# Opening of a two-layer hybrid trunk: order of the first loads, and where the split x tiles and h are made

## The reference

```python
h = concatenate([meta, x])                      # (272, 1024)
for l in range(2):
    f = (silu(a @ w_gate) * (a @ w_up)) @ w_down        # a = rms_norm(h, ffn1_pre[l]); 1024 -> 2816 -> 1024
    h = h + 0.5 * rms_norm(f, ffn1_post[l])
    proj = rms_norm(h, mix_pre[l]) @ w_in[l]
    mix = [pool | short convolution | gated linear attention](proj) @ w_out[l]
    h = h + rms_norm(mix, mix_post[l])
    h = h + 0.5 * rms_norm(swiglu(rms_norm(h, ffn2_pre[l])), ffn2_post[l])
return h[16:]
```

## Time and profile before

| | |
|---|---|
| median of the runs | 1014.23 us |
| the profiled execution, its own time | 1014.0 us |
| its span, first to last instruction | 1012.2 us |
| mean granted TensorE clock | 0.998 |
| TensorE busy | 1001.2 us (99%), 8904 matmuls |
| VectorE busy | 628.4 us (62%) |
| ScalarE busy | 499.5 us (49%) |
| GpSimd busy | 259.9 us (26%) |
| share of TensorE in the chain that ended last | 96% |
| SyncE's first issues | x0 0.76, meta 1.72, x1 2.11, weights from 2.57 us |
| landings | meta 5.42, x1 7.21, first weight piece 7.95, unit 1 13.57 us |

### The profile page before, as it was taken

How to read it: one execution, slowest core, us unless ns; L and a number is a source line. 1 busy time by engine, 2 the same in 40 slices (tenths; PEclk the granted TensorE clock), 3 DMA queues, 4 the chain that set the end, 5 groups by cost and what they waited for, 6 DMA issues and landing times.

```text
span 1012.2 us, 21339 instructions
## 1 busy us (share of the span) xinstructions
PE 1001.2 (99%) x8904; PEld 977.9 (97%) x8904; DVE 628.4 (62%) x643; ACT 499.5 (49%) x564; POOL 259.9 (26%) x180
## 2 busy tenths in 40 slices
PE   8999999999999999999999999999999999999997
PEld 7999999999999999999999999999999999999885
DVE  5765453588967745544477455444889787555485
ACT  6553443566566544343555443435675665434331
POOL 0343330113401333330103333301125014333200
PEclk9999999999999999999999999999999999999999
DMA  9775535645454755436747654357453547666521
GB/s 312 222 225 166 163 131 187 217 128 166 127 168 151 232 185 166 130 115 194 227 129 227 190 167 130 114 190 231 127 167 127 173 146 250 186 189 203 189 82 42
DMA packets 164019, 173.87 MB, mean 172 GB/s; under 512 B 9454, under 2 KB 151014, under 8 KB 163958
## 3 DMA queue, kind: packets, MB, share of 16 engines
q1 hardware_dynamic: 162044, 171.28, 53.4%
q10 hardware_dynamic: 1914, 1.72, 0.6%
HBM read 171.91 MB, written 1.06 MB: 171 GB/s over the span
## 4 chain that ended last, share of the span: by engine, by line
PE 96%; DMA 1%; DVE 1%; ACT 1%; SPq 0%; issue 0%; ACTq 0%; POOL 0%; DVEq 0%; POOLq 0%
PE ps L1477 25%; PE ps L1479 25%; PE ps L1478 25%; PE ps L1509 2%; PE ps L1494 2%; PE ps L1510 2%; PE ps L1685 2%; PE ps L1684 2%; PE ps L1686 2%; PE ps L1618 2%; PE ps L1656 2%; PE ps L1657 2%; PE ps L1811 1%; DMA raw<-in_ffn_wu 1%; PE ps L1536 1%; DVE w_lo L896 0%
## 5 line engine op out<-in xcount | busy, mean ns | idle before, releaser
L896 DVE TENSOR_TENSOR w_lo<-raw,w_hi 128x2048 fp32r<-128x2048 f32 (+2 forms) x174 | 383.8, 2210 | 269.1 <-ACT w_hi L578 268.5
L1477 PE MATMUL ps<-x_hi,w_hi 128*128 128x272 f32 (+2 forms) x1608 | 462.2, 287 | 0.7 <-DVE w_lo L896 0.7
L1479 PE MATMUL ps<-x_hi,w_lo 128*128 128x272 f32 (+2 forms) x1608 | 460.3, 286 | 0.0
L1478 PE MATMUL ps<-x_lo,w_hi 128*128 128x272 f32 (+2 forms) x1584 | 453.1, 286 | 0.0
L578 ACT ACTIVATE w_hi<-raw 128x2048 fp32r<-128x2048 f32 (+2 forms) x174 | 310.9, 1790 | 202.7 <-PE ps L1479 143.7
L1477 PEld LDWEIGHTS ps<-x_hi,w_hi 128*128 128x128 f32 x1608 | 302.8, 188 | 3.2 <-DVE w_lo L896 1.1
L1479 PEld LDWEIGHTS ps<-x_hi,w_lo 128*128 128x128 f32 x1608 | 302.3, 188 | 0.0
L1478 PEld LDWEIGHTS ps<-x_lo,w_hi 128*128 128x128 f32 x1584 | 298.3, 188 | 0.0
L1391 POOL TENSOR_TENSOR up<-gate,up 128x544 f32<-128x544 f32 (+1 forms) x44 | 59.4, 1350 | 311.8 <-ACT gate L713 311.8
L1394 POOL TENSOR_TENSOR hid_lo<-up,hid_hi 128x544 f32 (+3 forms) x44 | 122.4, 2782 | 45.5 <-ACT hid_hi L717 45.5
L713 ACT ACTIVATE gate<-gate 128x544 f32<-128x544 f32 (+1 forms) x44 | 28.7, 653 | 197.2 <-DVE gate L1112 197.2
(11 more groups left out here) (233 smaller groups left out, 1103.4 us busy)
## 6 DMA issues: line engine op xcount, KB each, us to landing
raw<-in_ffn_wg SPq DMA_DIRECT2D x87, 512.0 KB, 4.0
raw<-in_ffn_wu SPq DMA_DIRECT2D x87, 512.0 KB, 4.9
raw<-in_ffn_wd SPq DMA_DIRECT2D x72, 384.0 KB, 3.2
raw<-in_w_in SPq DMA_DIRECT2D x40, 512.0 KB, 4.6
raw<-in_ffn_wd SPq DMA_DIRECT2D x20, 512.0 KB, 4.7
raw<-in_ffn_wd SPq DMA_DIRECT2D x28, 256.0 KB, 3.3
raw<-in_w_out SPq DMA_DIRECT2D x12, 512.0 KB, 4.9
raw<-in_w_out SPq DMA_DIRECT2D x8, 256.0 KB, 3.9
```

The costliest lines, as they stand in the source:

```text
L896: v_.tensor_tensor(w_lo[:, slot, 0:n], raw[:, slot, 0:n], f32(w_hi[:, slot, 0:n]), ALU.subtract)\
L1477: pe.matmul(out_, wh, xh, start=first, stop=False)
L1478: pe.matmul(out_, wh, xl, start=False, stop=False)
L1479: return pe.matmul(out_, wl, xh, start=False, stop=last)
```

## The change

- SyncE issues meta first, once, with a broadcast that writes it to both halves of `meta_tok` (32 rows), then x0 and x1. GpSimd's memset of `meta_tok` and the wait on it are gone.
- x_hi and x_lo of the token columns of x are made straight from the transposes in PSUM (`turned`), tile by tile. VectorE's and ScalarE's copies of h that stood in between are gone.
- The 16 meta columns of x_hi and x_lo are made apart, for all eight tiles at once: VectorE multiplies by the gains into `meta_scaled`, ScalarE copies it to x_hi, VectorE subtracts.
- h is copied out of PSUM by ScalarE, two tiles at a time, after the w_hi of unit 2 (`whole_h`), each copy once VectorE has made x_lo of its tiles. Behind them, before the squares of x1, stand the squares of the meta rows, which were the first thing on ScalarE.
- TensorE takes the 96 products in another order (pairs of feature tiles: high products first, then w_lo, then x_lo) and waits for h of all tiles before unit 2.

```diff
@@ sync, first_unit @@
+                sp.dma_start(meta_tok[:, :], meta.unsqueeze(0).to_broadcast([2, NMETA, D])).then_inc(meta_in, 16)
                 for tt in range(2):
-                    if tt:
-                        sp.wait_ge(meta_set, 1)
-                        sp.dma_start(meta_tok[0:NMETA, :], meta).then_inc(meta_in, 16)
                     sp.dma_start(x_tok[:, tt, :], x[0, tt * P:(tt + 1) * P, :]).then_inc(x_in[tt], 16)
@@ before the blocks @@
+        def turned(kk):
+
+            return ps[:, 4 + kk // 2, 2 * P * (kk % 2):2 * P * (kk % 2 + 1)]
@@ scalar @@
             def high_x(kk):
-                act.wait_ge(h_ready, kk + 1)
-                act.activation(x_hi[:, kk, :], h[:, kk, :], ACT.Copy, scale=col("ffn1_pre", 0, kk)).then_inc(xh_ready, 1)
-
-            def high_h(kk):
-                act.wait_ge(ends_tr, 2 + kk + 1)
+                act.wait_ge(ends_tr, 1 + 2 * (kk // 2 + 1))
+                act.activation(x_hi[:, kk, NMETA:T], turned(kk), ACT.Copy, scale=col("ffn1_pre", 0, kk)).then_inc(xh_ready, 1)
+
+            def whole_h(kk):
+                act.wait_ge(xl_ready, kk + 2)
                 src = ps[:, 4 + kk // 2, :].rearrange("p (k t) -> p k t", k=2)
                 act.activation(h[:, kk:kk + 2, NMETA:T], src, ACT.Copy).then_inc(h_ready, 2)
...
+            act.wait_ge(x_in[0], 16)
+            x_squares(0, x_tok[:, 0, :], f_flat[:, 0:D])
+            act.wait_ge(meta_x, 1)
+            act.activation(x_hi[:, :, 0:NMETA], meta_scaled[:, :, :], ACT.Copy).then_inc(meta_hi, 1)
+            act.wait_ge(par_ready, 1)
+            high_x(0)
+            high_part(0, 0, 1, first_in, 32, first_hi)
+            high_x(1)
+            high_part(0, 1, 1, second_in, 32, first_hi)
+            high_x(2)
+            high_part(0, 2, 2, raw_in[0], 32, unit_hi)
+            high_x(3)
+            high_x(4)
+            high_x(5)
+            high_part(1, 0, 2, raw_in[1], 32, first_hi)
+            high_x(6)
+            high_x(7)
+            high_part(1, 2, 2, raw_in[1], 32, unit_hi)
+            high_unit(2, UNIT)
+            for kk in range(0, KT, 2):
+                whole_h(kk)
             act.wait_ge(meta_in, 16)
             x_squares(2, meta_tok[0:NMETA, :], f_flat[0:NMETA, D:2 * D])
-            act.wait_ge(x_in[0], 16)
-            x_squares(0, x_tok[:, 0, :], f_flat[:, 0:D])
-            high_part(0, 0, 1, first_in, 32, first_hi)
-            act.wait_ge(par_ready, 1)
-            act.wait_ge(meta_h, 4)
-            high_x(0)
...
-            high_unit(2, UNIT)
             act.wait_ge(x_in[1], 16)
             x_squares(1, x_tok[:, 1, :], x_tok[:, 1, :])
@@ vector @@
+            v_.wait_ge(par_ready, 1)
+            gains = par[:, C["ffn1_pre"][0]:C["ffn1_pre"][0] + KT].unsqueeze(2).to_broadcast([P, KT, NMETA])
+            v_.tensor_tensor(meta_scaled[:, :, :], h[:, :, 0:NMETA], gains, ALU.mult).then_inc(meta_x, 1)
+            v_.wait_ge(meta_hi, 1)
+            v_.tensor_tensor(x_lo[:, :, 0:NMETA], meta_scaled[:, :, :], f32(x_hi[:, :, 0:NMETA]), ALU.subtract)\
+              .then_inc(meta_lo, 1)
 
             def low_x(kk):
-                v_.wait_ge(meta_h, 4)
-                v_.wait_ge(xh_ready, kk + 1)
-                v_.scalar_tensor_tensor(x_lo[:, kk, :], h[:, kk, :], col("ffn1_pre", 0, kk),
-                                        f32(x_hi[:, kk, :]), ALU.mult, ALU.subtract).then_inc(xl_ready, 1)
-            first_h(0, 1)
-            first_h(1, 1)
+                v_.wait_ge(xh_ready, 2 * (kk // 2 + 1))
+                v_.scalar_tensor_tensor(x_lo[:, kk, NMETA:T], turned(kk), col("ffn1_pre", 0, kk),
+                                        f32(x_hi[:, kk, NMETA:T]), ALU.mult, ALU.subtract).then_inc(xl_ready, 1)
             low_part(0, 0, 1, first_hi, 1, first_lo)
             low_x(0)
-            first_h(2, 2)
+            low_x(1)
             low_part(0, 1, 1, first_hi, 2, first_lo)
-            low_x(1)
             low_part(0, 2, 2, unit_hi, 1, unit_lo)
@@ gpsimd @@
-            pool.memset(meta_tok[:, :], 0.0).then_inc(meta_set, 1)
@@ tensor, first_units @@
+                    pe.wait_ge(par_ready, 1)
+                    pe.wait_ge(meta_hi, 1)
+                    first(0)
+                    second(0, True)
+                    first(1)
+                    second(0, False)
+                    second(1, False)
+                    second(1, True)
+                    for k2 in range(2, KT, 2):
+                        first(k2)
+                        first(k2 + 1)
+                        second(k2, True)
+                        second(k2 + 1, True)
+                        second(k2, False)
+                        last = second(k2 + 1, False)
+                        if k2 % 4 == 2:
                             last.then_inc(unit_used, 1)
+                    pe.wait_ge(h_ready, KT)
```

More of the change, by code:

```diff
@@ L198, in trunk @@
         meta_tok = place("meta_tok", [2 * NMETA, D])
+        meta_scaled = place("meta_scaled", [P, KT, NMETA])
         par_rows = sq_odd[:, 0, 0:P]
@@ L251, in trunk @@
         meta_in = sem("meta_in")
-        meta_set = sem("meta_set")
+        meta_x = sem("meta_x")
+        meta_hi = sem("meta_hi")
+        meta_lo = sem("meta_lo")
         meta_h = sem("meta_h")
@@ L1051, in _ @@
             v_.wait_ge(meta_in, 16)
-            v_.wait_ge(meta_set, 1)
             for i in range(4):
@@ L1058, in _ @@
             v_.tensor_copy(par[:, 0:n_first], ps[:, 2, 0:n_first]).then_inc(par_ready, 1)
[L1060 to L1063, removed]
-            def low_x(kk):
-                v_.wait_ge(meta_h, 4)
-                v_.wait_ge(xh_ready, kk + 1)
-                v_.scalar_tensor_tensor(x_lo[:, kk, :], h[:, kk, :], col("ffn1_pre", 0, kk),
-                                        f32(x_hi[:, kk, :]), ALU.mult, ALU.subtract).then_inc(xl_ready, 1)
-            first_h(0, 1)
-            first_h(1, 1)
+            v_.wait_ge(par_ready, 1)
[4 more added lines that the diff above has]
+              .then_inc(meta_lo, 1)
+            def low_x(kk):
+                v_.wait_ge(xh_ready, 2 * (kk // 2 + 1))
+                v_.scalar_tensor_tensor(x_lo[:, kk, NMETA:T], turned(kk), col("ffn1_pre", 0, kk),
+                                        f32(x_hi[:, kk, NMETA:T]), ALU.mult, ALU.subtract).then_inc(xl_ready, 1)
             low_part(0, 0, 1, first_hi, 1, first_lo)
             low_x(0)
-            first_h(2, 2)
+            low_x(1)
             low_part(0, 1, 1, first_hi, 2, first_lo)
-            low_x(1)
             low_part(0, 2, 2, unit_hi, 1, unit_lo)
@@ L1629, in products, with second, first @@
                         return last
[L1630 to L1633, removed]
+                    def second(kg, of_w):
+                        if of_w:
+                            if lows_[kg]:
+                                pe.wait_ge(*lows_[kg])
+                            return products(w_lo, x_hi, kg)
+                        pe.wait_ge(meta_lo, 1)
+                        pe.wait_ge(xl_ready, kg + 1)
+                        return products(w_hi, x_lo, kg)
+                    def first(kg):
                         pe.wait_ge(xh_ready, kg + 1)
@@ L1637, in first_units @@
                         products(w_hi, x_hi, kg)
[L1638 to L1643, removed]
+                    highs = ((first_hi, 1), (first_hi, 2), (unit_hi, 1), None, (first_hi, 3), None, (unit_hi, 2), None)
+                    lows_ = ((first_lo, 1), (first_lo, 2), (unit_lo, 1 + RING), None, (first_lo, 3), None, (unit_lo, 2 + RING), None)
+                    pe.wait_ge(par_ready, 1)
[14 more added lines that the diff above has]
+                        if k2 % 4 == 2:
                             last.then_inc(unit_used, 1)
+                    pe.wait_ge(h_ready, KT)
                 if bnd == 0:
```

## The result

The changed kernel takes 1017.90 us (median of 7 runs, 1017.03 to 1018.53), the kernel before 1014.16 (7 runs): a ratio of 1.0035, 95% interval [1.0026, 1.0045], 3.7 us more. The forecast was 1014.9 with 1013.5 to 1016.4 around it, most likely inside 0.2%. The direction was right and the time far outside the range.

The account below looks back on a forecast made before the run. TensorE is the bound, with room only before unit 3 (28.69 us), held there by the norm chain through ScalarE and VectorE. That chain ends 0.7 later: 1014.2 + 0.7 = 1014.9 us, range 1013.5 to 1016.4.

Parts of the forecast that it names:

- Loads: Opening DMA loads: with meta first and no memset wait, all later landings come 0.4 us earlier, unit 2 at 16.13.
- nothing (the hole moves elsewhere): Lower bound on the lead of later landings: the hole in the DMA rate behind x0, about 0.4 us, only moves.
- ScalarE's chain: ScalarE from w_hi of unit 2 at 16.13 to the root's end at 22.38, against 20.88 before: 1.50 us later.
- the slack of 0.8: Before the reciprocal: the root waited for VectorE's w_lo of unit 2 until 21.84, so 0.8 us of ScalarE's lateness is absorbed.
- The start of TensorE: TensorE's opening: x1 lands at about 6.8 and the first product comes at 8.45 us against 9.28.
- Still before the first product: Meta pieces in the opening: even if meta landed at the old time, they would end near 8.2 us, before TensorE's products.
- x_hi from PSUM: ScalarE's price for 256 columns without meta: taken as 0.41 us, with bounds below 0.41 and up to 0.58.
- Unit 4 2 us early: Behind unit 3: unit 4 is asked for at 35.4; its w_lo, some 0.7 us later, would still be 2 us early.
- Rival A: TensorE's clock falls in the 2.4 us gap before unit 3: slower, 1016.4 us, or 1021 at the dear end; chance 0.12.
- Rival B: ScalarE's queue is no longer than before, stores at 0.44 each and lead 0.6: 1014.0 us; chance 0.08.
- Rival C: The norm chain does not bind unit 3; TensorE reaches it at 26.65: 1012.2 us, 2.0 less; chance 0.06.
- Rival D: The loads do nothing: x1 still lands at 7.2, unit 3 0.4 later than forecast, 1015.3 us; counted within the forecast's 0.74.

Follow-up runs that it names:

- e4: The changed kernel with meta's one 128 KB load laid out as 32 copies of row 0 instead of 2 copies of 16 rows: 1015.60 us, ratio 1.0015.
- e2: The kernel before with only the new loads (meta first by one broadcast into 32 rows, no memset): 1017.06 us, ratio 1.0028.
- e3: The changed kernel with meta loaded by two plain loads of 16 rows each instead of the broadcast: 1014.72 us, ratio 1.0007.
- e9: e7 with the w_hi of unit 4 also moved ahead of the wait for the stores' landing: 1014.28 us, ratio 1.0002.
- e1: The changed kernel with the loads of before, all its compute changes kept: 1015.21 us, ratio 1.0013.
- e7: The kernel before with only ScalarE's w_hi of unit 3 moved ahead of the three stores of the norms: 1013.89 us, ratio 0.9998.
- e8: e6 with the root and reciprocal moved early and GpSimd issuing the stores and load of the norms: 1011.98 us, ratio 0.9981.
- e5: e3 with the squares of the meta rows back at the head of ScalarE's program: 1013.17 us, ratio 0.9991.
- e6: e5 with the squares of x1 moved into ScalarE's wait for unit 1: 1012.73 us, ratio 0.9986.

## Why the prediction was wrong, point by point

- **The step that failed is the first one, "Loads".** It took the lead of all later landings as 0.4, between nothing and 0.6. It measured minus 2.7 (unit 2 at 19.20 for 16.53). The lower bound "nothing (the hole moves elsewhere)" was no bound: the new load was priced by its bytes, 64 KB more at 350 GB/s, and its issue by the plain load's row, and no row of before shows a broadcast of two. The rule quoted under e4 speaks against it, and the prediction did not weigh it. What the runs show in its place: the loads cost 2.8 us (e2), because two of the 16 shares of every later load come after the broadcast (e4). With two plain loads (e3) x1 is read at 6.93, 0.3 earlier than before, and the time is 1014.72, near the forecast's 1014.9. In part that is luck: unit 2 lands at 16.73 there and not at 16.13, unit 3 starts at 29.93 and not at 29.4, and the profiled execution took 1015.09. Even the lead of 0.4 can't be told from scatter: with the loads of before unit 2 is there at 16.5 in the kernel before and e9, at 16.1 in e1 and 16.2 in e7, and with two plain loads between 15.9 (e8) and 16.9 (e5).
- **ScalarE's chain was right.** 6.25 from the w_hi of unit 2 to the end of the root, 6.23 measured; the copies of h 1.90 for 1.92; the slack of 0.8 behind VectorE's w_lo of unit 2 used up. e1, where unit 2 by luck is read at 16.13 exactly as forecast (its loads are the old ones), has its root end at 22.37 (22.38) and unit 3 at 29.33 (29.4).
- **The start of TensorE was off** beyond the lateness of the loads: 8.60 for 8.45 in e3, but 9.22 in e1, where meta lands at its old time. "Still before the first product" overlooked that ScalarE's copy of the meta columns stands ahead of all of its x_hi. It cost nothing, as the chain behind binds.
- **x_hi from PSUM** measured 0.46 to 0.47 for 256 columns, 0.36 from start to start (two between 17.15 and 17.86); 0.41 was taken.
- **Nothing behind unit 3 took anything back**: 983.7 us for 983.5.
- **"Unit 4 2 us early" was read too kindly.** w_lo of unit 4 was early; the up product, which TensorE also waits for, ended at 34.0 before with unit 4 asked for at 34.7 (e7 and e6 make it late).
- **Rival A**: the wait before unit 3 was 1.7 us in the kernel after and 2.5 in e3, and the clock stayed at 1.00 in both. It fell elsewhere, see below. **Rival B** fell with the stores: the first two still took 1.60 us together (25.91 in the kernel after), and the lead was not there. **Rival C** was real, but for another kernel (e8). **Rival D** was the right thought with the wrong size: the loads did worse than nothing.

## What to carry to other kernels

A DMA is not priced by its bytes. One whose access pattern begins with a short dimension, as a broadcast of two copies, can take over twice as long as two plain loads and holds up whatever is queued behind it; give a load many rows outermost, or issue it twice. And when work is moved from an engine's idle start to its late program, ask which chain stands behind it there: 1.04 us of squares that cost nothing at 5.5 us cost 1.0 behind the w_hi of unit 2. After one chain is shortened, look for the next of about the same length before expecting the gain.

## What was not expected of the hardware

TensorE's clock fell in the opening of the kernel after. Windows of its profile, columns as above:

```profile
6.00:8.70 2.70, 0.20 (x1) 0.13 (x1) 1.12 (x3) 0.00 (x1) 0.00 (x0) 1.00 1.04 304
...
9.30:12.60 3.30, 3.19 (x15) 2.47 (x14) 1.42 (x5) 2.49 (x7) 0.00 (x0) 0.52 1.10 348
12.60:14.00 1.40, 1.40 (x12) 1.40 (x11) 1.40 (x4) 1.40 (x3) 0.00 (x0) 0.92 1.10 348
```

From the end of the warm products (5.4) to x0's transposes at 8.72 TensorE had one small transpose to do; then its clock was 0.52 of full on the mean of 9.3 to 12.6, the lower level of 1.2 GHz, while it worked, and returned by itself. The 16 transposes of x took 3.43 us in place of twice 1.09. It cost the end nothing: e2 shows the same fall (0.57 from 8 to 10, 0.58 from 10 to 12), and its time is 2.8 up with its landings 2.8 late; and in e4, 2.3 us below this kernel, the 16 transposes are no faster (3.68 us). The Trainium skill, "TensorE: Matmul & The Clock Gate", Part 1, describes such a fall after idleness and the return under load; this trace agrees with both directions. Whether a fall in a later gap is what scatters single runs of the kernels with a long wait before unit 3 was not shown by any profile and stays open. The record leans both ways: e1's three runs of 1016.80 to 1016.87 have a mean granted clock of 0.997 or 0.998 and its other eight 0.998 or 0.999, but e7, without a wait before unit 3, has a run of 1016.26 at 0.999.
